# Loads of z behind the next chunk's loads in SyncE's queue, and a semaphore of its own for B and C, in the SSD output phase

## The reference

```python
# per direction, chunks of 128 tokens, 16 heads of 64 channels in 4 groups
seg    = a_cs[:, :, :, None] - a_cs[:, :, None, :]
decay  = exp(where(lower_tri, seg, -inf))
scores = einsum("bcqgn,bcsgn->bcqsg", cmat, bmat)
y_diag = einsum("bcqsg,bcqsgr,bcsgrp->bcqgrp", scores, decay, xdt)
y_off  = einsum("bcqgn,bcgrpn,bcqgr->bcqgrp", cmat, start_states, exp(a_cs))
y      = y_diag + y_off
# summed over both directions, plus d_skip * x; then
g = y * silu(z)
```

## Time and profile before

| | us |
|---|---|
| median of 3 executions | 4014.41 |
| lowest and highest | 4010.56, 4015.59 |
| profiled execution, own time | 4012.46 |
| span of the profiled execution | 4010.7 |
| PE busy in the span | 3676.8 (92%) |
| SSD output phase in the span (first load to last `gated`) | 3058.6 to 3410.2 |

### The profile page before, as it was taken

How to read it: one execution, slowest core, us unless ns; L and a number is a source line. 1 busy time by engine, 2 the same in 40 slices (tenths; PEclk the granted TensorE clock), 3 DMA queues, 4 the chain that set the end, 5 groups by cost and what they waited for, 6 DMA issues and landing times. The chain is left out here.

```text
span 4010.7 us, 44395 instructions
## 1 busy us (share of the span) xinstructions
PE 3676.8 (92%) x16946; PEld 2984.5 (74%) x16946; DVE 1705.7 (43%) x2042; ACT 1201.0 (30%) x2339; POOL 982.8 (25%) x465
## 2 busy tenths in 40 slices
PE   6799999999999999996799899999856888799998
PEld 2688888888888888884599677777645777688886
DVE  5544420001434330003644455455376666566662
ACT  3311111111010111112377455554203553333332
POOL 0021112121222221211000100101057554444442
PEclk8899999999999999997899999999788899899998
DMA  7533322121111121217999857856486543655552
GB/s 259 168 105 120 113 86 78 63 78 63 68 73 68 73 79 63 78 52 266 301 300 275 184 126 166 194 129 154 122 302 222 158 145 124 224 188 191 202 194 103
DMA packets 386934, 597.39 MB, mean 149 GB/s; under 512 B 152019, under 2 KB 238979, under 8 KB 374395
## 3 DMA queue, kind: packets, MB, share of 16 engines
q1 hardware_dynamic: 297229, 403.94, 33.4%
q10 hardware_dynamic: 80336, 157.83, 10.3%
q0 software_dynamic: 9216, 33.56, 3.7%
HBM read 392.22 MB, written 203.03 MB: 148 GB/s over the span
## 5 line engine op out<-in xcount | busy, mean ns | idle before, releaser
L579 PE MATMUL pl_bank<-hl_hi,pl_w_hi 128*128 128x512 f32 x2336 | 923.9, 396 | 19.1 <-POOL pl_w_lo L550 19.1
L580 PE MATMUL pl_bank<-hl_lo,pl_w_hi 128*128 128x512 f32 x2336 | 922.7, 395 | 0.0
L581 PE MATMUL pl_bank<-hl_hi,pl_w_lo 128*128 128x512 f32 x2336 | 922.5, 395 | 0.0
L579 PEld LDWEIGHTS pl_bank<-hl_hi,pl_w_hi 128*128 128x128 f32 x2336 | 440.7, 189 | 121.8 <-issue 19.4
L581 PEld LDWEIGHTS pl_bank<-hl_hi,pl_w_lo 128*128 128x128 f32 x2336 | 440.7, 189 | 103.0
L580 PEld LDWEIGHTS pl_bank<-hl_lo,pl_w_hi 128*128 128x128 f32 x2336 | 440.8, 189 | 102.4
L547 POOL TENSOR_TENSOR pl_w_hi<-pl_w,pl_zero 128x1024 fp32r<-128x1024 f32 x73 | 138.1, 1892 | 1280.8 <-PE pl_bank L581 1276.1
L655 DVE TENSOR_SCALAR pl_res<-pl_raw,pl_taps 128x2048 f32<-128x2048 f32 x40 | 85.5, 2139 | 775.3 <-ACT pl_raw L605 775.3
L1760 PE MATMUL mo_bank<-mo_hi,mo_w_hi 128*128 128x512 f32 x768 | 305.5, 398 | 22.9 <-POOL mo_w_lo L1732 18.5
L1732 POOL TENSOR_TENSOR mo_w_lo<-mo_w,mo_w_hi 128x1024 fp32r<-128x1024 f32 x96 | 237.8, 2479 | 278.1 <-ACT mo_w_hi L1803 278.1
L1762 PE MATMUL mo_bank<-mo_hi,mo_w_lo 128*128 128x512 f32 x768 | 300.5, 391 | 0.0
(11 more groups left out here) (205 smaller groups left out, 5725.9 us busy)
## 6 DMA issues: line engine op xcount, KB each, us to landing
conv_spec<-spec_s SPq DMA_DIRECT2D x248, 256.0 KB, 6.3
mo_w<-in_w_br SPq DMA_DIRECT2D x96, 512.0 KB, 3.7
pl_w<-in_w_rec SPq DMA_DIRECT2D x73, 512.0 KB, 3.2
kern_s<-taps_res SPq DMA_DIRECT2D x16, 2048.0 KB, 7.0
spec_xin<-kern_s SPq DMA_DIRECT2D x64, 512.0 KB, 5.5
spec_s<-spec_res ACTq DMA_DIRECT2D x128, 256.0 KB, 4.1
st_xb<-tok_s SPq DMA_DIRECT2D x36, 768.0 KB, 7.3
u_s<-pl_res ACTq DMA_DIRECT2D x24, 1024.0 KB, 3.9
```

The costliest lines, as they stand in the source:

```text
L579: pe.matmul(out, w_hi[:, q, m], h_hi[:, k, r], start=(k == 0), stop=False)
L580: pe.matmul(out, w_hi[:, q, m], h_lo[:, k, r], start=False, stop=False)
L581: mm = pe.matmul(out, w_lo[:, q, m], h_hi[:, k, r], start=False, stop=(k == KT - 1))
```

## The change

The four loads of a chunk are issued in another order: `bc`, `x`, `st` of chunk c, then `z` of chunk c-1. The wait for `s_res` goes with the load of z. The last z is loaded behind the loop. `bc` raises a new pair of semaphores `s_bc`; `s_ld` is raised by `x` alone. PE's `scores(c)` waits for `s_bc`, POOL's `inputs(c)` for `s_ld`.

```diff
@@ -1368,7 +1368,7 @@
-        s_ld, s_stl, s_zl, s_gst = ph.sems("ld", 2), ph.sems("stl", 2), ph.sems("zl", 2), ph.sems("gst", 2)
+        s_bc, s_ld, s_stl, s_zl, s_gst = ph.sems("bc_in", 2), ph.sems("ld", 2), ph.sems("stl", 2), ph.sems("zl", 2), ph.sems("gst", 2)
@@ -1382,18 +1382,23 @@
         @block.sync
         def _(sp):
+            def load_z(c):
+                if c >= 2:
+                    sp.wait_ge(s_res, 2 * c - 2)
+                sp.dma_start(z[:, c % 2], z_v[:, :, c * P:(c + 1) * P]).then_inc(s_zl[c % 2], 16)
+
             for c in range(NCH):
                 q, at = c % 2, slice(c * P, (c + 1) * P)
                 if c >= 2:
                     sp.wait_ge(s_offm, 4 * c - 4)
-                sp.dma_start(bc[:, q], bc_v[:, :, at]).then_inc(s_ld[q], 16)
+                sp.dma_start(bc[:, q], bc_v[:, :, at]).then_inc(s_bc[q], 16)
                 if c >= 2:
                     sp.wait_ge(s_xdt, 3 * c - 3)
                 sp.dma_start(x[:, q, :], x_v[c + NCC, :, 0:D]).then_inc(s_ld[q], 16)
                 sp.dma_start(st[:, q], st_v[c]).then_inc(s_stl[q], 16)
-                if c >= 2:
-                    sp.wait_ge(s_res, 2 * c - 2)
-                sp.dma_start(z[:, q], z_v[:, :, at]).then_inc(s_zl[q], 16)
+                if c:
+                    load_z(c - 1)
+            load_z(NCH - 1)
@@ -1406,7 +1411,7 @@
             def inputs(c):
-                pool.wait_ge(s_ld[c % 2], 32 * (c // 2) + 32)
+                pool.wait_ge(s_ld[c % 2], 16 * (c // 2) + 16)
@@ -1428,7 +1433,7 @@
             def scores(c):
                 q = c % 2
-                pe.wait_ge(s_ld[q], 32 * (c // 2) + 32)
+                pe.wait_ge(s_bc[q], 16 * (c // 2) + 16)
```

## The result

The changed kernel took 4017.21 us (median of 17 runs, 4010.71 to 4027.51) against 4010.56 us before (17 runs on the same chip, 4006.50 to 4015.85). The ratio is 1.0017, with a 95% interval of 1.0010 to 1.0024: 6.65 us slower, between 4.0 and 9.6. The prediction was 4014 us, within a range of 3990 to 4023 us, and counted on a change of -0.5 us. The measured time lies in that range, but a part of this is luck: the forecast stood on 4014.41 us for the kernel before, the median of three executions, which seventeen put at 4010.56. A gain of next to nothing was forecast, and the change costs a little.

A forecast was written before the change was run, and what follows sets the result against it. In the SSD output phase, the wait for z holds back bc and x. Removing twelve waits (-31.1 us) leaves six pairs, 253.6 against 254.06: -0.5 us, 4012.46 to 4012.0; with 1.95 us to the median, 4014 us, range 3990 to 4023.

The forecast's parts named there:

- What bounds: SSD output phase: SyncE's wait before loading z holds back bc and x; PE waits 38.4 us in 13 places.
- Queue and semaphore: SyncE's loads: scores' loads land 5 us or more early, z costs nothing, the semaphore gives 0; twelve waits go, -31.1 us alone.
- What is late next: Output loop without x waits: POOL delays DVE's sums, PE waits 1.85 us for weigh; 20.07 us an iteration at full clock.
- the collision: DVE's two sums reading SBUF twice are held until POOL's inputs operations end, losing 3.11 us together in an iteration.
- The reading that a wait for x puts the sums behind POOL: Kernel before: while PE and DVE stand, POOL runs on, so DVE's sums come behind most or all of its work.
- The sum: Twelve output iterations: six pairs of 23.50 + 18.76 = 42.26 us make 253.6 us against 254.06 now, -0.5 us.
- The iteration behind such a one is another case: Output iteration after a 23.50 us one with a clock fall: no wait for weigh, so it takes 18.76 us.
- the alternation: Output iterations alternate between some 23.5 us, with a low clock, and 18.8 us; chance 0.48, range 4006 to 4021 us.
- The time before: The kernel before's twelve output iterations, between scores at 3119.82 and 3373.88, take 254.06 us, 21.17 us each.
- A: Rival: PE's clock holds through its waits for weigh, iterations take 20.07 us; -13.2 us, 4001 us; chance 0.15.
- B: Rival: DVE's sums slip past POOL, the 31.1 us come nearly whole; 3983 us, with a part 3990; chance 0.15.
- C: Rival: clock falls at the third segments' start, iterations take 24.91 us; +8.0 us, 4022 us for six pairs; chance 0.14.

The follow-up runs named there:

- e1_order_only: Changed kernel with PE's scores waiting for both bc and x again, so only the load order differs from before: 4020.11 us against 4011.81, ratio 1.0020.
- e2_sem_only: Kernel before with only the separate semaphore for bc added, z still loaded ahead of the next chunk's loads: 4008.54 us, ratio 0.9995.
- e3_pool_waits: Changed kernel with POOL's inputs of the next chunk held until DVE has made both sums of the current one: 3968.69 us, ratio 0.9892.
- e6_sums_late: Changed kernel with DVE's two sums moved later, behind gated and behind weigh, POOL untouched: 3973.60 us, ratio 0.9899.
- e4_fill: Changed kernel with seven unused 512-column matmuls added on PE ahead of the third segments, where it waits for weigh: 4000.61 us, ratio 0.9970.
- e8: Changed kernel unaltered, run again for a second profile: 4017.33 us against 4014.06 for the kernel before, ratio 1.0010.
- e10: Changed kernel unaltered, run once for a third profile: 4011.88 us.

## Why the prediction was wrong, point by point

- **What bounds.** Right: the wait for z held the loads back, and with the new order no load behind the first is late.
- **Queue and semaphore.** Right in kind. The loads land over 5 us ahead, z is never late, and in e1_order_only and e2_sem_only the semaphore gives nothing that the medians can tell. x lands sooner than I took, at 4.9 us.
- **What is late next.** Right in the main: the collision and the wait for `weigh` are there in every iteration that begins at full clock. The wait is 1.85 us in most and 1.06 to 1.78 in the others, and where the clock stays up the iteration takes 20.07 us, or 19.3 to 19.6 with the shorter wait. e3_pool_waits and e6_sums_late take the meeting away from either side, and 27 to 32 us come with it, counted from e4_fill, where the clock stays up. The reading that a wait for x puts the sums behind POOL was half right: in the twelve iterations of the first profile of before no second sum is held, but the first takes 1.4 to 2.9 us in eight, and the granted clock is below 1 in ten. The full iteration was put at 18.2 us without it and is 18.0.
- **The sum: the step that failed.** "The iteration behind such a one is another case" was taken for every long iteration, so that pairs of 42.26 us made -0.5 us. A short iteration came only where the low stretch reached the next `scores`, 4, 3 and 3 times in the three profiles and not six. In the profile e8, 23.26 is followed by 23.22 us, and the twelve come to 257.9 us, not 253.6; the three profiles of the changed kernel average 255.8. That term was 2.2 us too low. For the same reason the waits went past the 12 us (`weigh`) and 15 us (`y_off`) of the forecast, to 19.0 and 23.9, and the alternation did not appear.
- **The time before.** The other term was read from one profile, 254.06 us; two more give 249.52 and 250.30 us. The mean is 2.8 us lower. The two errors together, 2.2 + 2.8 = 5.0 us, turn -0.5 into the +4.5 us that the profiles show in the twelve iterations, inside the interval of the 6.65 us measured; the phase as a whole shows 3.2. With 251.3 us for before, even the predicted alternation is a loss of 2.3 us. Both terms could have been given a spread; I carried one sample of each, for a difference that was smaller than either.
- **The rivals.** A (the clock holds) was 4001 us, -13.2 us; e4_fill, where PE is kept busy, took 4000.6, -11.2 against its own runs of before, so its price was near and its condition false. B (the sums slip past POOL) needed DVE's sum to come earlier against `scores` than in the sample. It does not: in full-clock iterations the first sum comes 7.78 us behind `scores`, in e3 as in the sampled one. C (the clock falls at the start of the third segments) was priced at 24.91 us an iteration; 24.8 to 24.9 us stand in the profile after, in three of thirteen iterations, mixed with all the others. So a part of C occurs, at a price below the one for all six pairs. (C's +8.0 us stands as +8.1 in the sum of the prediction; the first is right.)

On the clock, removing one wait of PE moved idle time to another place, between the diagonal matmuls, and the clock was no higher for it: over 3119 to 3374 us the mean granted clock is 0.90, 0.88 and 0.90 in the three profiles of the changed kernel (after, e8, e10) and 0.92, 0.92 and 0.91 in those of before. The Trainium skill ("TensorE: Matmul & The Clock Gate", section "What's actually happening") has activity lift the clock. That agrees with e4_fill, where activity put into the wait kept it at full speed (1.00 in every iteration from the third on).

What makes the clock fall at a given wait stays open. In the changed kernel the wait of 1.85 us for `weigh` is followed by a low stretch in most iterations and by none in others (3158.20 to 3178.27 above), in e2_sem_only three waits of 1.85 us are followed by none, and in these profiles the wait of 1.70 us for `y_off` is never followed by one. e4_fill shows only that filling the wait keeps the clock up.

## What to carry to other kernels

When a wait goes, look at what ran in its shadow: here POOL finished its work while PE and DVE stood, and without the wait DVE's sums met it. Hold the engine with slack back by a wait, or move the operations that read two tensors from SBUF to a place where the other engine is idle, and do it together with the earlier loads: the POOL wait alone gave -16 us, the earlier loads alone +7, both -43. A forecast of a few us out of a loop whose iterations differ by 6 us needs several profiles of before.

## What the runs showed of the hardware that was not expected

With another order, the same transfers land faster. Issues of the profile after (KB each, median us to landing), against the earlier trace rows:

```profile
y_x<-tok_s SPq DMA_DIRECT2D x16, 512.0 KB, 4.9
y_z<-z_s SPq DMA_DIRECT2D x16, 512.0 KB, 4.0
ym_s<-y_res ACTq DMA_DIRECT2D x16, 512.0 KB, 3.2
y_bc<-xbc_s SPq DMA_DIRECT2D x15, 512.0 KB, 4.0
```

and the store of before:

```profile
ym_s<-y_res ACTq DMA_DIRECT2D x16, 512.0 KB, 7.8
```

The store of the results landed in 3.2 us where it took 7.8 before, x in 4.9 instead of 6.7, `bc` in 4.0 instead of 5.5. In the round of the earlier trace rows the store was issued at 3221.31, 4.4 us behind z and with three loads between them; in the round of the changed kernel shown above it went out at 3243.76, 6.6 us behind z and with nothing between. That the spacing is the cause is a reading; no run changes it alone. Nothing here waited for the store.

The lengths of the iterations can repeat from one execution to another: those of e1_order_only and e8_after_again agree one by one within 0.05 us over all thirteen, falls of the clock included, though both vary between 18.8 and 24.9 us. How the clock's falls come to lie the same way in two executions, and another way in the first profile of the changed kernel, stays open.
